# Feed-forward gate and upper projection with seven block products, sums on chip, weight sums on GpSimd

## What is computed

```python
    x = x + rms_norm(mix, g_mix_post)
    hf = rms_norm(x, g_ffn_pre)
    f = (jax.nn.silu(hf @ w_gate) * (hf @ w_up)) @ w_down
    x = x + rms_norm(f, g_ffn_post)
```

## Time and profile before

| | us |
|---|---|
| median of 3 runs | 2916.38 (2911.19 to 2919.33) |
| the profiled execution, its own time | 2911.99 |
| its span | 2910.2 |
| TensorE busy (share of the span) | 2745.2 (94%) |
| VectorE busy | 1240.3 (43%) |
| ScalarE busy | 882.0 (30%) |
| GpSimd busy | 206.3 (7%) |
| feed-forward stage, start to end of the span | 1452.34 to 2910.2 |

### The profile page before, as it was taken

One profiled execution on the slowest core, in us unless ns is written; L12 is line 12 of the kernel. 1 busy time (PEld: TensorE's weight loads), 2 busy tenths in 40 slices (PEclk: granted clock), 3 DMA queues, 4 the chain that ended last, 5 costly groups with the idle time before them and its releaser, 6 DMA issues.

```text
span 2910.2 us, 48239 instructions
## 1 busy us (share of the span) xinstructions
PE 2745.2 (94%) x17582; PEld 1575.6 (54%) x17770; DVE 1240.3 (43%) x3050; ACT 882.0 (30%) x2196; POOL 206.3 (7%) x568
## 2 busy tenths in 40 slices
PE   7998887989999999989899999999999999999998
PEld 6666665648676675845444444444444444444443
DVE  6335676746666666677622122121122121122144
ACT  6116787434444444433322002120012110022111
POOL 2001121002111121211100000000000000000000
PEclk9999998999999999899999999999999999999999
DMA  5123345420111101144220131012321013211044
GB/s 193 66 73 71 77 96 154 149 69 29 48 31 31 39 23 59 63 152 150 90 75 29 51 105 39 27 43 87 134 62 40 25 57 133 92 44 48 10 152 177
DMA packets 176175, 224.97 MB, mean 77 GB/s; under 512 B 12829, under 2 KB 143848, under 8 KB 175360
## 3 DMA queue, kind: packets, MB, share of 16 engines
q1 hardware_dynamic: 174810, 219.84, 24.0%
q0 software_dynamic: 1200, 2.97, 0.4%
HBM read 156.85 MB, written 65.92 MB: 77 GB/s over the span
## 4 chain that ended last, share of the span: by engine, by line
PE 49%; issue 1%; DVE 0%; ACT 0%; POOLq 0%; POOL 0%; ACTq 0%
PE f_ps_y L115 6%; PE f_ps_y L113 6%; PE f_ps_gate L114 6%; PE f_ps_y L114 5%; PE f_ps_up L115 5%; PE f_ps_up L114 5%; PE f_ps_up L113 5%; PE f_ps_gate L115 5%; PE f_ps_gate L113 5%; DVE f_total L2667 0%; DVE f_w_lo L2616 0%; DVE f_total L2661 0%; DVE f_x L2671 0%; ACT f_w_hi L2558 0%; ACT f_squares L2594 0%
## 5 line engine op out<-in xcount | busy, mean ns | idle before, releaser
L2629 DVE TENSOR_TENSOR f_hidden<-f_silu,f_ps_up 128x512 f32<-128x512 f32 (+1 forms) x110 | 65.2, 593 | 625.2 <-ACT f_silu L2570 625.2
L114 PE MATMUL f_ps_gate<-act_lo,f_w_hi 128*128 128x512 bf16 (+1 forms) x858 | 277.5, 342 | 11.7 <-DVE f_hidden L2629 5.6
L114 PE MATMUL f_ps_y<-f_down_lo,f_h_hi 128*128 128x512 bf16 (+1 forms) x727 | 276.3, 380 | 9.4 <-issue 7.0
L115 PE MATMUL f_ps_up<-act_hi,f_w_lo 128*128 128x512 bf16 (+1 forms) x880 | 284.7, 342 | 0.0
L114 PE MATMUL f_ps_up<-act_lo,f_w_hi 128*128 128x512 bf16 (+1 forms) x880 | 284.7, 342 | 0.0
L113 PE MATMUL f_ps_up<-act_hi,f_w_hi 128*128 128x512 bf16 (+1 forms) x880 | 284.6, 342 | 0.0
L113 PE MATMUL f_ps_y<-f_down_hi,f_h_hi 128*128 128x512 bf16 (+1 forms) x744 | 282.9, 380 | 0.5
L115 PE MATMUL f_ps_y<-f_down_hi,f_h_lo 128*128 128x512 bf16 (+1 forms) x738 | 280.6, 380 | 1.1
L115 PE MATMUL f_ps_gate<-act_hi,f_w_lo 128*128 128x512 bf16 (+1 forms) x858 | 277.4, 342 | 1.2
L113 PE MATMUL f_ps_gate<-act_hi,f_w_hi 128*128 128x512 bf16 (+1 forms) x836 | 269.0, 341 | 1.2
L2570 ACT ACTIVATE f_silu<-f_ps_gate 128x512 f32<-128x512 f32 (+1 forms) x110 | 57.1, 519 | 653.7 <-PE f_ps_up L115 653.7
(11 more groups left out here) (410 smaller groups left out, 5463.8 us busy)
## 6 DMA issues: line engine op xcount, KB each, us to landing
y_part_rows<-f_total SPq DMA_DIRECT2D x48, 512.0 KB, 2.6
f_total<-y_part_rows SPq DMA_DIRECT2D x48, 512.0 KB, 3.5
m_w_raw<-in_w_gate SPq DMA_DIRECT2D x22, 512.0 KB, 5.3
f_raw_up<-in_w_up SPq DMA_DIRECT2D x22, 512.0 KB, 6.3
f_raw_down<-in_w_down SPq DMA_DIRECT2D x22, 512.0 KB, 3.4
m_w_raw<-in_w_in SPq DMA_DIRECT2D x20, 512.0 KB, 5.8
nx<-in_x_prompt SPq DMA_DIRECT2D x16, 512.0 KB, 3.4
o_x<-in_x_prompt SPq DMA_DIRECT2D x16, 512.0 KB, 4.7
```

The source lines that it names most:

```text
L114: pe.matmul(out, w_hi, x_lo, start=False, stop=False)
L115: return pe.matmul(out, w_lo, x_hi, start=False, stop=last)
L2629: nc.vector.tensor_tensor(hidden[u][:, 0:n], act_out[u][:, 0:n], ps_up[u][:, 0:n], ALU.mult).then_inc(hidden_done, 1)
```

## The change

The gate and the upper projection of a hidden tile are together a matrix of two block rows (gate, up) and two block columns (the upper and lower half of the 1024 inputs, 4 x 128 rows each). The input of two token chunks of 512 is a matrix of 2 x 2 blocks too (input half, token chunk). Before, the eight block products are made one by one. After, seven are made, of sums and differences of blocks (A11, S1, S2, A12, S3, S4, A22 of the weights with B11, T1, T2, B21, T3, B22, T4 of the tokens), and the four results are put together from them.

- The 2048 prompt tokens are two pairs of chunks. The 22 hidden tiles are gone through once for each pair: 44 units (`unit`) of seven products of 12 matmuls. The 64 samples are multiplied in the units of the first pair, four blocks as before, 48 matmuls of 64 columns a unit, with the weights A11, S1, A12 and A22; their banks lie in the second buffer of `ps_y`. All weights are loaded and split for each pair.
- `w_sum_up` makes the four sums S1 to S4 of the weight blocks on GpSimd, 512 columns each; `t_sum_of` makes T1, T3, T2 and T4 of the token blocks, 2048 columns each, once for each pair. T2 and T4 use T1's place and wait for its split.
- Seven weight blocks of 512 columns are split for each unit, on ScalarE and VectorE, one unit ahead, in place of two of 1024. A weight's buffer is single but for A22, so it is split again after the product that reads it.
- ScalarE copies three intermediate banks to SBUF (`near`, `mid`, `away`) and VectorE adds three banks to them. NEAR is the first token chunk of a pair, AWAY the second.
- A part is two hidden tiles in place of four or six: `down` runs 11 times for each pair, over nine token tiles (eight and the samples) in the first pair and eight in the second, AWAY rows first. The running sum stays on chip, in the place of the transposed input (`x32`), which is kept in float32; `y_part_rows` is gone.
- In `stage_mix_out` VectorE's `keep_low` goes, and ScalarE's copy writes float32; the token blocks are split at the start of `stage_ffn` and between the pairs.
- The first pair's rows and the samples are finished (root, scale, x1, store) during the second pair's parts, one tile after each; the second pair's in its last part.
- Everything is written out, without loops.

The diff, cut to what is spoken of (the indentation within the stages is reduced):

```diff
-        def keep_high(t, s, n):
+        def keep_turned(t, s, n):
             act.wait_ge(turned_ready, t + 1)
-            nc.scalar.activation(g.act_hi[:, :, ds(t * P, n)], turned[s][:, :, 0:n], ACT.Copy).then_inc(hi_done, 1)
+            nc.scalar.activation(g.x32[:, :, ds(t * P, n)], turned[s][:, :, 0:n], ACT.Copy).then_inc(turned_free, 1)
...
-        def keep_low(t, s, n):
-            dve.wait_ge(hi_done, t + 1)
-            cols = ds(t * P, n)
-            nc.vector.tensor_tensor(g.act_lo[:, :, cols], turned[s][:, :, 0:n], g.act_hi[:, :, cols],
-                                    ALU.subtract).then_inc(turned_free, 1)
...
+PART = 2
+PARTS = HIDDEN_TILES // PART
+UNITS = N_PAIRS * HIDDEN_TILES
+PRODUCTS = 7
+A11, S1, S2, A12, S3, S4, A22 = range(PRODUCTS)
+B11, T1, T2, B21, T3, B22, T4 = range(PRODUCTS)
+W_ORDER = [A11, A22, S1, S2, A12, S3, S4]
+X_S1, X_S2, X_SD = range(PRODUCTS, PRODUCTS + 3)
+SUM_ORDER = [[T1, T3, X_SD, T2, T4], [T1, T3, T2, T4]]
+T_ORDER = [[B11, X_S1, T1, X_S2, B21, T3, T2, B22, X_SD, T4], [B11, T1, B21, T3, T2, B22, T4]]
+DOWN_ORDER = list(range(PAIR_TILES // 2, PAIR_TILES)) + list(range(PAIR_TILES // 2))
...
+        w_sum = {j: sb(f"f_w_sum{j}", [P, HK, P]) for j in (S1, S2, S3, S4)}
...
+        x1_area = sb("f_sums_then_x1", [P, 2 * D_MODEL])
...
+                sp.wait_ge(w_sums, 4 * u)
+                sp.wait_ge(w_low, w_at(u - 1, A22))
+            sp.dma_start(raw_up[:, :, :], g.w_up[:, m * P:(m + 1) * P].rearrange("(k p) c -> p k c", p=P)).then_inc(up_in, 16)
...
+            m = u % HIDDEN_TILES
+            sp.wait_ge(w_low, w_at(u - 1, A12))
+            sp.dma_start(raw_gate[:, :, :], g.w_gate[:, m * P:(m + 1) * P].rearrange("(k p) c -> p k c", p=P)).then_inc(gate_in, 16)
...
+        def multiply(u, j, bank, first):
+            q = pair_of(u)
+            pe.wait_ge(w_low, w_at(u, j))
+            if u % HIDDEN_TILES == 0:
+                pe.wait_ge(t_low, t_at(q, j))
+            for k in range(HK):
+                high, low = w_hi[j][u % 2][:, k, :], w_lo[j][u % 2][:, k, :]
+                nc.tensor.matmul(bank[:, :], high, t_hi[j][:, k, :], start=first and k == 0, stop=False, skip_group_check=True)
+                nc.tensor.matmul(bank[:, :], high, t_lo[j][:, k, :], start=False, stop=False, skip_group_check=True)
+                mm = nc.tensor.matmul(bank[:, :], low, t_hi[j][:, k, :], start=False, stop=k == HK - 1, skip_group_check=True)
+            return mm
...
+        def unit(u):
+            sample = pair_of(u) == 0
+            one = bank1[u % 2]
+            if u >= 2:
+                pe.wait_ge(hidden_done, row_at(u - 2, NEAR))
+            mm = multiply(u, A11, one, True)
+            if sample:
+                if u % PART:
+                    pe.wait_ge(hidden_done, row_at(u - 1, SAMPLE))
+                elif u:
+                    pe.wait_ge(total_done, down_at(0, u // PART))
+                mm = multiply_sample(u, A11, X_S1, s_gate_ps, True, False)
+            mm.then_inc(p_done, 1)
+            if u:
+                pe.wait_ge(combined, 3 * u)
+            mm = multiply(u, S1, bank3, True)
+            if sample:
+                mm = multiply_sample(u, S1, X_S1, s_up_ps, True, False)
+            mm.then_inc(p_done, 1)
+            pe.wait_ge(kept, 3 * u + 1)
+            multiply(u, S2, one, False).then_inc(p_done, 1)
+            mm = multiply(u, A12, bank2, True)
...
+            mm.then_inc(p_done, 1)
+            pe.wait_ge(kept, 3 * u + 3)
+            multiply(u, S3, one, False).then_inc(p_done, 1)
+            multiply(u, S4, bank3, False).then_inc(p_done, 1)
+            pe.wait_ge(combined, 3 * u + 2)
+            mm = multiply(u, A22, one, False)
+            if sample:
+                mm = multiply_sample(u, A22, X_SD, s_up_ps, False, True)
...
+        def down(q, part):
+            u = q * HIDDEN_TILES + part * PART + PART - 1
+            pe.wait_ge(down_low, u + 1)
+            for n in range(n_down[q]):
+                rows = down_rows(n)
+                size = NSAMP if rows == SAMPLE else P
...
+                pe.wait_ge(h_done, row_at(u, rows))
+                if n == 1 and q == 0:
+                    pe.wait_ge(hidden_done, row_at(u, SAMPLE))
+                if down_at(q, part) + n >= 2:
+                    pe.wait_ge(total_done, down_at(q, part) + n - 1)
...
+            nc.scalar.activation(near[v][:, :], bank1[v][:, :], ACT.Copy).then_inc(kept, 1)
+            if more:
+                w_split(u + 1, A11)
+                w_split(u + 1, A22)
+            act.wait_ge(p_done, made(u, S1))
+            if u > HIDDEN_TILES and v == 0:
+                act.wait_ge(ss_done, min(u % HIDDEN_TILES // PART, PAIR_TILES + 1))
+            nc.scalar.activation(mid[v][:, :], bank3[:, :], ACT.Copy).then_inc(kept, 1)
+            if more:
+                w_split(u + 1, S1)
+            act.wait_ge(p_done, made(u, S2))
+            nc.scalar.activation(away[v][:, :], bank1[v][:, :], ACT.Copy).then_inc(kept, 1)
+            if more:
+                w_split(u + 1, S2)
...
+            act.wait_ge(combined, 3 * u + 1)
+            nc.scalar.activation(near[v][:, :], near[v][:, :], ACT.Silu).then_inc(silu_done, 1)
+            if more:
+                w_split(u + 1, A12)
+                w_split(u + 1, S3)
+            act.wait_ge(combined, 3 * u + 3)
+            nc.scalar.activation(away[v][:, :], away[v][:, :], ACT.Silu).then_inc(silu_done, 1)
+            if more:
+                w_split(u + 1, S4)
+            keep_high(u, AWAY, away[v][:, :])
+            if sample:
+                act.wait_ge(p_done, made(u, A22))
+                if u:
+                    act.wait_ge(h_done, row_at(u - 1, SAMPLE))
+                nc.scalar.activation(s_gate[:, :], s_gate_ps, ACT.Silu).then_inc(silu_done, 1)
+            keep_high(u, NEAR, near[v][:, :])
+            if sample:
...
+        def w_sum_up(u):
+            if u:
+                pool.wait_ge(w_low, w_at(u - 1, S4))
+            pool.wait_ge(up_in, 16 * (u + 1))
+            pool.wait_ge(gate_in, 16 * (u + 1))
+            nc.gpsimd.tensor_tensor(w_sum[S1][:, :, :], up1, up2, ALU.add).then_inc(w_sums, 1)
+            pool.wait_ge(w_sums, 4 * u + 1)
+            nc.gpsimd.tensor_tensor(w_sum[S2][:, :, :], w_sum[S1][:, :, :], gate1, ALU.subtract).then_inc(w_sums, 1)
+            nc.gpsimd.tensor_tensor(w_sum[S3][:, :, :], gate1, up1, ALU.subtract).then_inc(w_sums, 1)
+            pool.wait_ge(w_sums, 4 * u + 2)
+            nc.gpsimd.tensor_tensor(w_sum[S4][:, :, :], gate2, w_sum[S2][:, :, :], ALU.subtract).then_inc(w_sums, 1)
...
+            if q:
+                pool.wait_ge(t_low, t_at(q - 1, T4))
+            nc.gpsimd.tensor_tensor(t_sum, x12, x11, ALU.subtract).then_inc(t_sums, 1)
+            pool.wait_ge(t_sums, sum_at(q, T1))
+            nc.gpsimd.tensor_tensor(x12, x22, x12, ALU.subtract).then_inc(t_sums, 1)
...
+            if q == 0:
+                w_sum_up(0)
+            pool.wait_ge(t_low, t_at(q, T1))
+            nc.gpsimd.tensor_tensor(t_sum, x22, t_sum, ALU.subtract).then_inc(t_sums, 1)
+            pool.wait_ge(t_low, t_at(q, T2))
+            nc.gpsimd.tensor_tensor(t_sum, x21, t_sum, ALU.subtract).then_inc(t_sums, 1)
...
+            for part in range(PARTS):
+                for i in range(PART):
+                    u = q * HIDDEN_TILES + part * PART + i
+                    if u + 1 < UNITS:
+                        w_sum_up(u + 1)
+                if q == 0 and part == PARTS - 1:
+                    t_sum_of(1)
...
+                w_split(u + 1, A11)
+                w_split(u + 1, A22)
+                w_split(u + 1, S1)
+                w_split(u + 1, S2)
+            down_split(u)
+            dve.wait_ge(kept, 3 * u + 1)
+            dve.wait_ge(p_done, made(u, A12))
+            nc.vector.tensor_tensor(near[v][:, :], bank2[:, :], near[v][:, :], ALU.add).then_inc(combined, 1)
+            if more:
+                w_split(u + 1, A12)
+            dve.wait_ge(kept, 3 * u + 2)
+            dve.wait_ge(p_done, made(u, S3))
+            nc.vector.tensor_tensor(mid[v][:, :], bank1[v][:, :], mid[v][:, :], ALU.add).then_inc(combined, 1)
+            if more:
+                w_split(u + 1, S3)
+            dve.wait_ge(kept, 3 * u + 3)
+            dve.wait_ge(p_done, made(u, S4))
+            nc.vector.tensor_tensor(away[v][:, :], bank3[:, :], away[v][:, :], ALU.add).then_inc(combined, 1)
+            if more:
+                w_split(u + 1, S4)
+            dve.wait_ge(silu_done, silu_at(u, AWAY))
+            nc.vector.tensor_tensor(away[v][:, :], mid[v][:, :], away[v][:, :], ALU.mult).then_inc(hidden_done, 1)
+            keep_low(u, AWAY, away[v][:, :])
+            dve.wait_ge(silu_done, silu_at(u, NEAR))
+            dve.wait_ge(p_done, made(u, A22))
+            nc.vector.tensor_tensor(near[v][:, :], bank1[v][:, :], near[v][:, :], ALU.mult).then_inc(hidden_done, 1)
+            if sample:
```

(36 more changed lines are left out.)

498 lines of the change are left out of this document (280 added, 218 removed).

## The result

The kernel before took 2916.38 us (median of 5 runs, 2909.94 to 2923.19), the changed one 2939.06 (2937.06 to 2945.92): the ratio is 1.0092, 95% interval 1.0076 to 1.0109. It is slower, by more than the 0.3% that the prediction said can be told. The forecast was 2913; the range to 2940 just holds the time. The profiled execution took 2945.92 us (span 2944.1, granted clock 0.965), 7 above its median. A second sample of the same kernel on another occasion gave the ratio 1.0092 again, and its profiled execution 2934.13.

A forecast was written before the change was run, and what follows sets the result against it. TensorE was taken to bound the kernel (busy 1425 of 1458 us in the feed-forward stage). Matmuls −114.0 and waits −7, against pauses, clock, samples, start, pair change and tail, summed to +1.4, or 2913 us; range 2865 to 2940.

The forecast's parts named there:

- The removed matmuls: Gate and upper projection: 4224 matmuls of 512 columns become 3696; 528 fewer at 0.216 us each, −114.0 us.
- SP's queue runs three weight loads per unit: Inside a unit: weight loads replace the y_part traffic with microseconds to spare, nothing stalls, cost 0; VectorE's add to mid has 1.6 us spare.
- a stall within the units: Named sign of error: a stall at a bank or a weight, repeated by 44 units; one of 1 us is 44 us.
- Start: Start of the feed-forward stage: token block sums and splits delay unit 0's S2 to 33.6 us; +23.6 us with mutual waits.
- Tail: Last part's eight tiles: VectorE needs 3.7 us each against 2.6 of matmuls; +7.8 us.
- The turn: Turn from upper to down projection, 22 instead of 4: pauses of 2.7 and 3.0 us, 62.4 − 9.4 now = +53 us.
- Samples: Odd units of the first pair: TensorE waits after A11 for VectorE's samples' product of the unit before, 11 x 0.98 = +10.8 us.
- Change of pairs: Between the token pairs: VectorE's splits among down tiles, and waits between GpSimd and VectorE; +13.6 us.
- clock: After pauses: nine of 22 followed by the 1.2 GHz level for eight matmuls, 1.7 us a time; +13.6 us.
- B: Rival: VectorE doesn't wait for GpSimd, turn pauses stay at 2.2 and 2.5 us; −41, 2871 us; chance 0.23.
- C: Rival: a GpSimd weight sum takes 2.0 us, twice the copy, pauses grow to 3.5 and 3.9; 2974 us; chance 0.12.
- A: Main forecast: GpSimd and VectorE wait for each other, removed matmuls are paid back in pauses; 2913 us; chance 0.42.

## Why the prediction was wrong, step by step

A wait in the table of waits counts from the recorded end of a matmul, 0.38 us after its start, and its slot is 0.2155. Each wait thus costs 0.16 us more than its row says; that was left out, and is in the figures below.

- **The removed matmuls** (-114) were right: a slot is 0.2155 us. The number of pauses was right too, and nearly every term has the sign that it was given. The sum still came out 26.6 us short.
- **"SP's queue runs three weight loads per unit ..., each with microseconds to spare. These cost nothing"** is the step that failed, with the 1.6 us to spare that it gave "VectorE's add to mid before A22". It looked at the loads and not at what stands ahead of them on SyncE, a reload that waits for a store; and it counted what the sums hold at the turns, at the start and between the pairs, but not in the splits of each unit (2.8 us stretched to 6.5). Together these made nine stops of 1.5 to 3.2 us, 18.7 us with the 0.16 each, in place of 0, at the very add that was called the tightest. The kernel with the reload moved took them away, and the one without sums all but 0.4 us. The prediction had named the form that its error would take ("a stall within the units"), but had looked up no row for it.
- **Start** (+23.6): T2's own time was right by 1 us, but S2 was taken to wait for T2 alone. It waited 9.0 us longer, for a copy queued on ScalarE. The two runs on its order show that this was one of several waits in a row: behind it stood an add and then the samples' product, both VectorE's. The bound is VectorE's work with the holds of the sums in it: the first turn comes 9.6 us later than the prediction's chain has it.
- **Tail** (+7.8): VectorE's 3.7 us per tile held for the first tiles (3.59 from 2902.97 on). The stores and reloads of x1, 5.4 us per tile, were not in the working: 9.0 us short. The kernel with more buffers took 9.7 us off the tail.
- **The turn** (+53): the chain was right, its price too high. The pauses cost 49.2 us in place of 62.4: neighbours on an engine overlap by 0.09 us twice in the chain, and GpSimd holds the low half by 0.3 us in the first pair, not 0.5, and in the second not at all but at one turn, as the sums come after it there.
- **Samples** (+10.8): 5.2.
- **Change of pairs** (+13.6) and **clock** (+13.6; 7 of 22 turns and not 9, but also some longer waits): right within 2 us together. The clock's part is in part luck: fewer turns were followed by the low clock than reckoned, and spells behind a stop and inside the change of pairs, which the term did not count, made up for it.
- **Steps between tiles**, of 0.1 to 0.3 us where one shape or bank follows another, some 7 us in all, were in no term.
- **GpSimd and VectorE.** That each waits for the other holds in both directions (1.62 for 0.69, 3.32 for 1.26), and B is out. The Trainium skill, "SBUF — State Buffer", section "Who interferes with whom", states this as a lock between VectorE's operations with two SBUF inputs and GpSimd's reads, and says that an operation with at most one SBUF input is free of it; the traces agree with both (0.69 at most beside the sums). C is out: a sum takes 1.26, not 2.0. The copy's 1.11 was the right neighbour, 12% low.

Put together: stops, start, tail and the steps between tiles were 44 us too little, the turn and the samples 19 too much, with 1 or 2 elsewhere. None of the rivals was the case that came. What came is A with its clash in a place where A had ruled out any cost in one sentence, and a late load that made it show.

## What to carry to other kernels

When an edit doubles the loads on a queue, read what already waits on that queue, a store's completion above all, and price a late load at each unit together with whatever else already eats the same margin: here neither the late load nor the held splits stopped TensorE alone. A pause repeated tens of times is worth more than its length: shorten it first, and judge other edits with it short, since with pauses of 2.2 us the clock takes back what they bring. Where a start is one engine's backlog, reordering only names another waiter; take work off the engine, or take away what holds it.
